# Hybrid convolution trunk on eight cores: a bank class per column tile in the first phase, b0 by block from weights loaded with x, sample block ahead of the last prompt block

## What is computed

```python
def hybrid_layer(x, buf_a, buf_b, norm_g, w_in, conv_a_w, conv_a_b, ln_a_g, ln_a_b, conv_b_w, w_out):
    h = rmsnorm(x, norm_g)
    p = jnp.einsum('btd,de->bte', h, w_in)                           # (B, T, D_IN)
    a_val, a_gate, z_a, gb, gc, hb, z_b = jnp.split(p, splits, axis=-1)
    u = a_val * jax.nn.sigmoid(a_gate)                               # GLU
    ca, new_a = causal_dwconv(u, buf_a, conv_a_w)                    # width 31
    ca = head_layernorm(ca + conv_a_b, ln_a_g, ln_a_b)
    y_a = jax.nn.silu(ca) * jax.nn.silu(z_a)
    v = gc * hb
    cb, new_b = causal_dwconv(v, buf_b, conv_b_w)                    # width 3
    y_b = gb * cb * jax.nn.silu(z_b)
    y = jnp.einsum('bte,ed->btd', jnp.concatenate([y_a, y_b], axis=-1), w_out)
    return x + y, new_a, new_b
```

## Time and profile before

| | |
|---|---|
| median of 3 runs (1099.78 to 1100.42) | 1100.13 us |
| profiled execution | 1101.54 us |
| its span, slowest core | 1100.0 us |
| TensorE busy | 1051.6 us (96%) |
| VectorE, ScalarE, GpSimd busy | 766.7, 636.0, 311.5 us |
| mean granted TensorE clock, core 1 | 0.989 |

### The profile page before, as it was taken

How to read it: one execution, slowest core, us unless ns; L and a number is a source line. 1 busy time by engine, 2 the same in 40 slices (tenths; PEclk the granted TensorE clock), 3 DMA queues, 4 the chain that set the end, 5 groups by cost and what they waited for, 6 DMA issues and landing times.

```text
span 1100.0 us, 21025 instructions; the slowest of 8 cores (1089.4 to 1100.0 us)
## 1 busy us (share of the span) xinstructions
PE 1051.6 (96%) x6810; PEld 519.5 (47%) x6810; DVE 766.7 (70%) x1530; ACT 636.0 (58%) x1035; POOL 311.5 (28%) x470
## 2 busy tenths in 40 slices
PE   5888999999999999799999999999999999989998
PEld 2334445445455544344454454545545554444465
DVE  3588777788888888343336689888888888862233
ACT  5863666777787656221144367777778666542232
POOL 6462122232231222022250232322223212123341
PEclk9899999999999999899999999999999999999999
DMA  9728667868777659635541857877766756941444
GB/s 221 195 43 147 87 126 128 137 105 141 136 103 140 111 89 182 139 126 182 193 148 22 159 73 129 159 127 136 138 121 95 141 90 92 192 106 38 144 160 176
DMA packets 185803, 142.44 MB, mean 129 GB/s; under 512 B 140000, under 2 KB 152160, under 8 KB 185632
## 3 DMA queue, kind: packets, MB, share of 16 engines
q0 software_dynamic: 34352, 54.97, 32.4%
q1 hardware_dynamic: 150816, 82.17, 29.2%
q10 hardware_dynamic: 528, 3.96, 1.0%
HBM read 149.08 MB, written 43.79 MB: 175 GB/s over the span
## 4 chain that ended last, share of the span: by engine, by line
PE 84%; DMA 9%; DVE 2%; issue 2%; ACT 2%; POOL 1%; DVEq 0%; ACTq 0%; POOLq 0%; SPq 0%
PE psb L720 50%; PE psb L970 29%; DMA wsl<-w_in_r 4%; DMA y_sb<-x_d 2%; PE psb L1076 2%; PE psb L1077 1%; PE psb L1406 1%; DMA scr_c<-big 1%; DMA big<-w_out_r 1%; DMA big<-scr_c 1%; DMA wsl<-w_out_r 1%; ACT tmp L758 0%; PE psb L1409 0%; POOL toep L1486 0%; DVE tmp L1250 0%
## 5 line engine op out<-in xcount | busy, mean ns | idle before, releaser
L720 PE MATMUL psb<-h_sb,wsl 128*128 128x512 bf16 (+1 forms) x2288 | 364.7, 309 | 11.7 <-DMA wsl<-w_in_r 4.6
L720 PEld LDWEIGHTS psb<-h_sb,wsl 128*128 128x128 bf16 x2288 | 168.7, 98 | 184.3 <-issue 22.7
L1323 DVE TENSOR_TENSOR xst<-xst,psb 128x512 f32<-128x512 f32 (+2 forms) x80 | 45.0, 567 | 137.2 <-PE psb L720 120.9
L1050 ACT ACTIVATE toep<-wt_sb 32x512 bf16<-32x512 bf16 x192 | 120.0, 626 | 24.6 <-PE psb L1077 14.8
L758 ACT ACTIVATE tmp<-xst 128x1024 bf16<-128x1024 f32 (+2 forms) x44 | 38.7, 881 | 155.2 <-DVE xst L1323 149.1
L1250 DVE SCALAR_TENSOR_TENSOR tmp<-vbuf,cw_b_sb,tmp 128x512 f32<-128x512 bf16 (+1 forms) x160 | 105.9, 662 | 21.0 <-ACT tmp L1247 14.6
L970 PE MATMUL psb<-h_sb,wsl 128*128 128x512 bf16 x464 | 117.3, 379 | 0.2 <-ACT tmp L1258 0.2
L970 PE MATMUL psb<-xst,wsum 128*128 128x512 bf16 x464 | 113.9, 379 | 2.9 <-ACT psb L978 1.3
L970 PE MATMUL psb<-h_sb,wsum 128*128 128x512 bf16 x464 | 112.5, 379 | 2.5 <-DVE psb L991 2.2
L708 POOL DMA_DIRECT2D wsl<-w_in_r x112 | 60.8, 546 | 171.1 <-PE psb L720 110.7
L766 POOL TENSOR_TENSOR tmp<-tmp 128x512 bf16<-128x512 bf16 (+2 forms) x40 | 38.2, 956 | 157.8 <-ACT tmp L758 157.6
(11 more groups left out here) (155 smaller groups left out, 1847.7 us busy)
## 6 DMA issues: line engine op xcount, KB each, us to landing
wsl<-w_in_r POOLq DMA_DIRECT2D x112, 256.0 KB, 5.7
scr_u<-u_sb SPq DMA_DIRECT2D x16, 704.0 KB, 5.7
up_sb<-scr_u SPq DMA_DIRECT2D x16, 704.0 KB, 6.5
scr_c<-big SPq DMA_DIRECT2D x16, 640.0 KB, 7.3
big<-scr_c SPq DMA_DIRECT2D x16, 640.0 KB, 5.8
wt_sb<-wt_d POOLq DMA_DIRECT2D x64, 128.0 KB, 4.0
xst<-x_d SPq DMA_DIRECT2D x16, 512.0 KB, 7.7
x_mid<-xst SPq DMA_DIRECT2D x16, 512.0 KB, 2.9
```

What stands on the lines that cost most here:

```text
L720: ins = e.matmul(bank(v, n), lhsT=l_(), rhs=r_(), start=(first and i == 0), stop=(last and i == len(pairs) - 1))
L1050: act((lambda e, p=p, c=c: e.activation(out=toep[p, tp.slot, :].rearrange("p (m x) -> p m x", x=128)[:, :, 32 * c:32 * c + 32], in_=wt_sb[ ...
L1323: x_op[0] = dve((lambda e: e.tensor_tensor(out=x.s(m, part), in0=x.s(m, part), in1=bank(v, n), op=ALU.add)), n, [v, xr], [xr], holds=x.hol ...
```

## The change

- First phase: each of g0, v0, g1, v1, c0, hb0 has a bank class of its own with one bank (`OWNCAPS`), and its ScalarE results have classes by tile, instead of one shared class. Blocks run 0 1 2 4 3 (`BLK0`). `FINISH` puts h of block 0 after block 2 and of block 1 after block 3.
- `START` loads x4 early, the c0 and hb0 weights later, and ends with w6 and w7: z_B and B of head 0, into the slot pair `wsum` (`w_load_home`).
- b0 runs right after the first phase through `by_block`: all of its 16 products on plain h, blocks in the order 0 4 1 2 3, with no weight sums; the T forms come after it.
- b4 of layer 0 goes from `pair` to `plain` (eight matmuls of 512 columns more).
- `TRL = 8`: the tree of the head norm stops at eight slices, and eight matmuls with `same` add them (192 matmuls of 80 columns more, 64 VectorE adds fewer).
- New `ORDER`, steps, keys, `OUTQ`, `ZQ`; planner numbers for x, u and weight transfers, `SLACK` 1.5 for 0.5.

```diff
-    "C0 b0 a1 Z0 b1 C1 P2 C2 Z1 P3 a2 P4 C3 b2 Z2 a3 P5 C4 b3 Z3 P6 C5 a4 Z4 Z5 C6 b4 P7 C7 a5 b5 a6 b6 Z6u0 a7 b7u1 Z7up",
-    "C0 b0 a1 b1 C1 P2 Z0 C2 P3 Z1 a2 P4 C3 b2 Z2 P5 C4 P6 a3 b3 Z3 C5 C6 a4 Z4 Z5 P7 b4 Z6 a5 b5 C7 a6 b6u0 a7 b7u1 Z7up",
+    "b0 C0 a1 C1 P2 C2 Z0 b1 P3 a2 Z1 P4 C3 C4 P5 Z2 b2 P6 a3 C5 b3 C6 Z3 P7 a4 Z4 Z5 b4 Z6 a5 C7 b5 a6 b6u0 a7 b7u1 Z7up",
+    "b0 C0 a1 C1 P2 Z0 b1 C2 Z1 P3 a2 P4 C3 C4 P5 b2 Z2 P6 a3 b3 C5 Z3 a4 C6 Z4 Z5 b4 P7 a5 C7 b5 a6 b6 a7 Z6u0 b7u1 Z7up",
...
-OUTQ = (0, 2, 1, 3, 4)
+OUTQ = (1, 2, 0, 4, 3)
...
-ZQ = (0, 4, 3, 2, 1)
+ZQ = (2, 1, 4, 3, 0)
+TRL = 8
+OWN = (True, False)
+XD = (2.0, 1.68, 0.6)
+BLK0 = (0, 1, 2, 4, 3)
+WXD = 1.9
+OWNCAPS = {"g0": 1, "v0": 1, "g1": 1, "v1": 1, "c0": 1, "hb0": 1}
...
-START = "u0 u1 t0 t1 w0 w1 x1 w2 w3 w4 x2 w5 x3 x4"
+START = "u0 u1 t0 t1 w0 w1 x1 w2 x4 w3 x2 w4 w5 x3 w6 w7"
+B0Q = (0, 4, 1, 2, 3)
 RAW_ACT = ()
-FINISH = {1: (0,), 3: (1,)}
+FINISH = {2: (0,), 3: (1,)}
...
-SLACK, SLACK_DMA, SLACK_FIRST, QUIET = 0.5, 3.5, 2.0, 40.0
+SLACK, SLACK_DMA, SLACK_FIRST, QUIET = 1.5, 3.5, 2.0, 40.0
...
+    def w_load_home(src, v, i):
+        w = WH(v, i)
+        nload[0] += 1
+        pooldma((lambda e: e.dma_start(out=wsum[:, v.slot, 1024 * i:1024 * i + 1024], in_=src)), 1.4, (), [w], f"w{nload[0] % 12}", pkt=0.173,
+                name="w", holds=[v])
+        return w
...
-        bg = proj(wg, q, split, name=f"g{j}.{q}")
-        th = p1_gate(j, q, bg, rv)
-        bv = proj(wv, q, split, name=f"v{j}.{q}")
+        own = OWN[l]
+        bg = proj(wg, q, split, f"g{j}" if own else "proj", name=f"g{j}.{q}")
+        th = p1_gate(j, q, bg, rv, f"g{j}" if own else None)
+        bv = proj(wv, q, split, f"v{j}" if own else "proj", name=f"v{j}.{q}")
...
-            dve((lambda e: e.tensor_tensor(out=big[:, dst.slot, 0:16, :], in0=big[:, src.slot, 0:16, :], in1=big[:, src.slot, 16:32, :],
-                                           op=ALU.add)), 1280, [src], [dst], rate=2, lock=True, name=f"tr{j}")
-            for h in (8, 4, 2):
...
+            for h in [h for h in (16, 8, 4, 2) if h >= TRL]:
...
+            for g in range(0, TRL, step):
+                mm("stat", b, CROW, [((lambda: same[:]), (lambda i=i: big[:, at.slot, i, :])) for i in range(g, g + step)], [at, same_r],
+                   first=g == 0, last=g + step == TRL, name=f"st{j}")
...
+    def by_block(w1, w2, f1, f2, nm, **kw):
+        for q in B0Q:
+            f1(q, proj(w1, q, name=f"{nm}0.{q}", **kw))
+            f2(q, proj(w2, q, name=f"{nm}1.{q}", **kw))
...
+        if w_b0:
+            y = Y()
+            pending.append((8, y))
+            pb_b(l, 0, y, w_b0)
+            t_forms(x_late)
```

More of the change, by code:

```diff
@@ L109, in __init__ @@
         self.ops = []
+class WH(Res):
+    def __init__(self, home, i):
+        super().__init__()
+        self.home, self.i = home, i
 class Pool:
@@ L565, in build_nc @@
     pools = {
-        "bank": Pool(8, CAPS, spare=None, clean=CLEAN),
+        "bank": Pool(8, {**CAPS, **OWNCAPS}, spare=None, clean=CLEAN),
         "w": Pool(NW, spare=None),
@@ L727, in proj @@
         step = KC // split
+        if isinstance(w, WH):
+            kw = {**kw, "holds": kw.get("holds", []) + [w.home]}
         for i in range(split):
@@ L856, in sv, with p1_gate @@
         return tm(v, n) if v.pool == "snap" else bank(v, n)
-    def p1_gate(j, q, bg, rv=None):
+    def p1_gate(j, q, bg, rv=None, cls=None):
         n = BLOCKS[q][1]
@@ L1092, in tree @@
         def tree(src, dst):
-            dve((lambda e: e.tensor_tensor(out=big[:, dst.slot, 0:16, :], in0=big[:, src.slot, 0:16, :], in1=big[:, src.slot, 16:32, :],
-                                           op=ALU.add)), 1280, [src], [dst], rate=2, lock=True, name=f"tr{j}")
-            for h in (8, 4, 2):
-                dve((lambda e, h=h: e.tensor_tensor(out=big[:, dst.slot, 0:h, :], in0=big[:, dst.slot, 0:h, :],
-                                                    in1=big[:, dst.slot, h:2 * h, :], op=ALU.add)), h * 80, [dst], [dst], rate=2, lock=True, name=f"tr{j}")
+            at = src
+            for h in [h for h in (16, 8, 4, 2) if h >= TRL]:
+                dve((lambda e, h=h, at=at: e.tensor_tensor(out=big[:, dst.slot, 0:h, :], in0=big[:, at.slot, 0:h, :],
+                                                           in1=big[:, at.slot, h:2 * h, :], op=ALU.add)), h * 80, [at], [dst], rate=2, lock=True, name=f"tr{j}")
+                at = dst
             b = V("bank", "conv")
-            mm("stat", b, CROW, [((lambda: same[:]), (lambda i=i: big[:, dst.slot, i, :])) for i in range(2)], [dst, same_r], name=f"st{j}")
+            step = min(TRL, 8)
+            for g in range(0, TRL, step):
+                mm("stat", b, CROW, [((lambda: same[:]), (lambda i=i: big[:, at.slot, i, :])) for i in range(g, g + step)], [at, same_r],
+                   first=g == 0, last=g + step == TRL, name=f"st{j}")
             return b
@@ L1206, in pb_a_block @@
     def pb_a_block(l, j, q, wc, wh_, split=1, rv=None):
-        bc = proj(wc, q, split, name=f"c{j}.{q}")
-        th = pb_c(l, j, q, bc, rv)
-        bh = proj(wh_, q, split, name=f"hb{j}.{q}")
+        own = OWN[l]
+        bc = proj(wc, q, split, f"c{j}" if own else "proj", name=f"c{j}.{q}")
+        th = pb_c(l, j, q, bc, rv, f"c{j}" if own else None)
+        bh = proj(wh_, q, split, f"hb{j}" if own else "proj", name=f"hb{j}.{q}")
         pb_h(l, j, q, bh, th)
@@ L1283, in pb_b @@
             f1, f2 = f1g, f2g
-        (pair if f"b{j}" in WK[l] else plain)(wz, wb, f1, f2, f"b{j}", **y.kw())
+        (by_block if ws else pair if f"b{j}" in WK[l] else plain)(wz, wb, f1, f2, f"b{j}", **y.kw())
     nx = [0]
@@ L1336, in load @@
             rr = rr or [R()]
-            pooldma((lambda e: e.dma_start(out=ap(0, 1024), in_=src)), 1.4, (), rr, f"w{nload[0] % 12}", pkt=0.173, name="wx", holds=[v] if v else [])
+            pooldma((lambda e: e.dma_start(out=ap(0, 1024), in_=src)), WXD, (), rr, f"w{nload[0] % 12}", pkt=0.173, name="wx", holds=[v] if v else [])
             return rr
@@ L1487, in build_nc @@
                     pools["toep"].prev[i] = [tz]
+                elif tok[0] == "w" and i >= 6:
+                    if i == 6:
+                        home = V("sum")
+                    w_b0.append(w_load_home(w_in_r[l, (48, 24)[i - 6]], home, i - 6))
                 elif tok[0] == "w":
@@ L1501, in build_nc @@
         raws = {}
-        for q in range(NB) if l == 0 else FIRSTQ:
+        seq = BLK0 if l == 0 else FIRSTQ
+        for at, q in enumerate(seq):
             sp = KC if (l == 0 and q < 4) else 1
             cur = rv if l == 0 and q in RAW else None
-            nxt = q + 1 if l == 0 and q + 1 < NB else None
+            nxt = seq[at + 1] if l == 0 and at + 1 < NB else None
             if nxt in RAW:
@@ L1526, in build_nc @@
             x0_arena[:] = []
-        if PAIRS:
+        if PAIRS and not w_b0:
             t_forms(x_late if l == 0 else ())
@@ L1562, in build_nc @@
         for tok in ORDER[l].split():
-            run(tok)
+            if not (tok == "b0" and w_b0):
+                run(tok)
             seen.add(tok[:2])
```

30 lines of the change are left out of this document (16 added, 14 removed).

## The result

The changed kernel takes 1088.71 us (median of 4 runs, 1086.38 to 1090.63), the kernel before on the same chip 1099.95 (1099.59 to 1100.42). The ratio is 0.9897, 95% interval 0.9877 to 0.9917: 11.3 us less, where 6.6 were forecast. The profiled execution of the changed kernel took 1088.93 us. In the first of the three chip jobs behind the experiments, cores 0 to 3 had a granted clock of only 0.93 to 0.95 in every kernel, so its comparisons are of cores 4 to 7, and it has no ratio.

The account below looks back on a forecast made before the run. TensorE, 96% busy, was taken as the bound. The terms 8.6 - 4.3 - 2.2 + 5.4 - 5.3 - 2.1 - 6.7 sum to -6.6 us, giving a median of 1093.5 us, range 1087 to 1100.

Parts of the forecast that it names:

- More matmuls: Head norm and b4 of layer 0: 192 80-column and eight 512-column matmuls more, none hidden, +8.6 us.
- The start: First phase, from 15 us: TensorE does 66 products instead of 40 before c0's weights stop it, -4.3 us.
- no wait on squares of 6 us in 15 to 38: Sign to look for at the start: TensorE's 6 us wait for squares of x is gone.
- The rest of the first phase: Old stretch up to 78.88 us: loses 1.2 idle and 1.0 of low clock, -2.2 us.
- the new wait: Block 3, now last: TensorE waits 3.6 us for its norm, then 1.8 of half clock, +5.4 us.
- b0's weights: Loaded with x: the 3.52 us wait at 78.88 and 1.8 of slow matmuls go, -5.3 us.
- b0 as filler: Before the first convolution: b0 and most of a1 cover u's transfers; waits of 1.61 and 1.45 go, -2.1 us.
- End of layer 0: Loads into big issued earlier: 8.2 us of wait and slow matmuls go, 1.5 left for new waits, -6.7 us.
- The rest: Other step orders and SLACK over 880 us, unpriced by the trace: taken as 0, bounds -5 and +10 us.
- Of the rivals, the first: First phase gives little: b0's product on block 0 waits for GpSimd's eighth finishing product; 1099 us, chance 0.15.
- The in-order queue of TensorE in the steady stretches: Slower case: waits come more often in the new order; 1114 us if idle time trebles, chance 0.09.
- Twice the price for 80 columns: Weight loads show behind 80-column matmuls, each above 0.036 us; at twice the rate +6.9, 1100.4 us, chance 0.02.

Follow-up runs that it names:

- st_double: Changed kernel, same order, each of the 32 series of eight 80-column statistic matmuls issued twice: mean span of cores 4 to 7 1089.0 us, +8.4.
- adds_back: Changed kernel, its order kept, two more VectorE additions per tree and two slices instead of eight through same: 1082.45 us, 0.9856 of the kernel before.
- front_only: Kernel before with the new first phase alone, planned anew: 1091.35 us, 0.9938 of the kernel before.
- front_old: Changed kernel with the first phase as it was before, planned anew: 1102.16 us, 1.0048 of the kernel before.
- Blk0_old: Changed kernel with first-phase blocks in order 0 1 2 3 4 again, planned anew: 0.9993 of the kernel before, against 0.9934 for the changed kernel.
- big_late: Changed kernel with two w_out loads into big at layer 0's end ten places later in GpSimd's queue: 1087.59 us, 0.9906 of the kernel before.
- trl2: Changed kernel with TRL = 2 instead of 8, all else planned anew: mean span of cores 4 to 7 1118.8 us, 38 more.

## Why the prediction was right, step by step

The direction was right and the size short by 4.8 us. The terms, against the marks:

- *More matmuls, +8.6.* Work grew by 8.6 us, and st_double prices an 80-column matmul at 0.033 us where 0.036 was taken. "None of that work can hide" held. That what VectorE loses "lies beside TensorE and is costed at nothing" did not: adds_back shows that the two additions per tree cost TensorE 3.7 us between the convolutions. The prediction had named it as a gain of part of the 10 us of the steady stretches, and left it out of the sum. It is the **first mis-sized term**: the net price of the eight slices is 2.7 us between the convolutions and 4.5 over the kernel, not 6.9.
- *The start, -4.3.* From 15 to 40 us the losses fell by 6.5, and this is the **second mis-sized term**. The sum counted the products that TensorE does earlier, 5.6 less 1.3, and nothing for the clock in the same stretch; but that was 0.78 to 0.91 on the eight cores before (0.86 on core 1) and is 1.00 on all of them now. The shape was right: the weights landed at 37.3 as forecast. The sign "no wait on squares of 6 us in 15 to 38" says nothing, since there was none before: the 6.0 us of the earlier trace rows are the wait for the first piece of x, which stayed.
- *The rest of the first phase, -2.2; the new wait, +5.4; b0's weights, -5.3*: together -2.1, measured -2.1 from 40 us to the first convolution. There was no wait for b0's weights, and 3.20 us of wait for the norm (3.6 forecast). The low clock behind it was sized 1.8; it measured 2.2 as the mean of four cores and 3.0 on the profiled one. The 1.8 was read off twelve matmuls, and here the clock stayed low for more. That the sum fits to 0.1 is partly luck, for a shorter wait and a dearer clock offset each other.
- *b0 as filler, -2.1*: the losses of leg 2 fell by 4.6. The whole change has two causes in it: the waits of 1.61 and 1.45 us went as forecast, and no new waits of VectorE's heap came. But front_only, which has b0 as filler and the old order behind it, gains nothing in leg 2, and front_old, with the new order and no filler, gains 3.1. So the larger part is the new order's, which the sum had at 0. Blk0_old agrees with this term's reason without isolating it: with the first convolution 40 matmuls earlier, waits for u, toep and weights appear.
- *End of layer 0, -6.7*: the losses from 425 to 500 us fell by 7.1, all that there was. The two errors in the term offset each other. The 8.2 that were to go were read off one core, whose wait of 5.64 us is 4.3 in the mean of eight (2.7 to 5.8), and the 1.5 left for a new wait wasn't needed (446 to 460 has none). The mechanism given ("these two loads are issued ahead") is true but not enough: big_late takes it away and loses 1.1 us, not 8.
- *The rest, 0 with bounds -5 and +10*: this is the **third mis-sized term**. Leg 3 lost 3 us less outside the end of layer 0, most of it in the first phase of layer 1, where waits of 0.9 us for GpSimd and 1.1 for a weight went (core 1). Leg 4 lost 0.7 less, and the last leg 2.9 more. The wait for a tile of w_out there, 2.0 us in the mean before, is 2.8 now, and two waits for ScalarE ahead of it take 2.5 us for 1.0 (TensorE before, then now):

```profile
975.54 0.22 PE L720 MATMUL psb<-y_sb,wsl 128*128 128x64 bf16 x2 [1.96 <-DMA wsl<-w_out_r]
```

```profile
960.25 0.22 PE L743 MATMUL psb<-y_sb,wsl 128*128 128x64 bf16 x2 [3.76 <-DMA wsl<-w_out_r]
```

The granted clock is 0.91 from 960 to 980 there. How much of what legs 2 to 4 gained beyond the forecast the shorter trees made, and how much the new order, isn't shown; adds_back bounds the trees' part at 3.7 us.

Of the rivals, the first (b0's product on block 0 waits for GpSimd's eighth finishing product) did not come here, since TensorE took b0 at 55.49 without a wait. In blk0_old that product waits 0.5 to 0.8 us on three cores, and the 1.93 us there are the same kind of wait one block on, b0's product on block 1. The in-order queue of TensorE in the steady stretches, the slower case, showed its size in trl2: 16.3 us for one convolution result. Twice the price for 80 columns, the case of the Trainium skill's Back-to-back issue gap (TensorE: Matmul & The Clock Gate), is excluded by st_double.

## What to carry to other kernels

Where the bound engine is 96% busy, count the work and the losses apart and by program position; the changed kernel bought 21 us of losses with 8.6 us of work. A shorter chain on an engine that is only 70% busy can still be worth time, because its length is what an in-order queue waits for; here taking 64 additions off it cost 6.9 us of matmuls and returned 2.4 to 3.7, so in this order the additions were the cheaper. To test one number of a planned kernel, keep the planner's order and edit it afterwards: replanning moved the time by 38 us for reasons of its own. Compare kernels that ran on the same chip: the ratio of one and the same pair of kernels was 0.9897 on one and 0.9934 on another. And before a wait in a list becomes a reason, look up in the timeline where it stands.
